# Sixty TensorE products into an unread PSUM bank behind the last product of a two-block transformer kernel

## What is computed

```python
def _sqrelu_mlp(h, w1, w2):
    return jnp.square(jax.nn.relu(h @ w1)) @ w2
...
        h = _rmsnorm_2(x, mlp_norm_g[layer])
        x = x + _sqrelu_mlp(h, mlp_w1[layer], mlp_w2[layer])
    return x
```

## Time and profile before

| | |
|---|---|
| median of 3 runs | 1064.75 us (1064.57 to 1065.28) |
| time of the profiled execution | 1063.91 us |
| its span, first to last instruction | 1062.1 us |
| granted TensorE clock, mean | 0.997 |
| TensorE busy with matmuls | 1044.7 us, 98% of the span |
| VectorE, ScalarE busy | 746.2 us, 548.7 us |

### The profile page before, as it was taken

How to read it: one execution, slowest core, us unless ns; L and a number is a source line. 1 busy time by engine, 2 the same in 40 slices (tenths; PEclk the granted TensorE clock), 3 DMA queues, 4 the chain that set the end, 5 groups by cost and what they waited for, 6 DMA issues and landing times.

```text
span 1062.1 us, 19331 instructions
## 1 busy us (share of the span) xinstructions
PE 1044.7 (98%) x7716; PEld 966.7 (91%) x7716; DVE 746.2 (70%) x810; ACT 548.7 (52%) x589; POOL 2.2 (0%) x5
## 2 busy tenths in 40 slices
PE   9999999999999999999999999999999999999998
PEld 7998897899999999989889999999898997888887
DVE  6855747768766666678767766666788987766673
ACT  6422536545644444465796444444576574454442
POOL 0000000000000000000000000000000000000000
PEclk8999999999999999999999999999999999999999
DMA  9794242345556666666416455456353444646531
GB/s 311 227 208 143 80 139 80 121 146 160 167 173 181 192 196 194 185 199 226 132 41 238 159 195 201 158 202 194 119 160 120 158 160 159 238 158 202 193 118 40
DMA packets 162589, 177.11 MB, mean 167 GB/s; under 512 B 4800, under 2 KB 148288, under 8 KB 162536
## 3 DMA queue, kind: packets, MB, share of 16 engines
q1 hardware_dynamic: 160704, 174.06, 51.3%
q10 hardware_dynamic: 1832, 2.30, 1.2%
HBM read 174.78 MB, written 1.57 MB: 166 GB/s over the span
## 4 chain that ended last, share of the span: by engine, by line
PE 82%; DVE 11%; ACT 4%; issue 1%; DMA 0%; SPq 0%; DVEq 0%; ACTq 0%
PE proj L466 38%; PE aux L910 13%; PE proj L476 10%; PE aux L932 8%; PE proj L475 5%; DVE wlo L1727 4%; DVE f L1727 2%; DVE f L1730 2%; ACT whi L1244 1%; DVE u L1730 1%; PE aux L663 1%; DVE x_all L1727 1%; PE aux L778 1%; PE aux L763 1%; PE aux L525 1%
## 5 line engine op out<-in xcount | busy, mean ns | idle before, releaser
L1727 DVE TENSOR_TENSOR wlo<-raw,whi 128x2048 fp32r<-128x2048 f32 (+2 forms) x179 | 374.7, 2093 | 99.8 <-ACT whi L1244 88.2
L466 PE MATMUL proj<-u,whi 128*128 128x256 f32 (+1 forms) x1888 | 346.9, 285 | 1.5 <-DVE u L1730 0.7
L1244 ACT ACTIVATE whi<-raw 128x2048 fp32r<-128x2048 f32 (+2 forms) x172 | 309.8, 1801 | 69.5 <-PE proj L466 43.2
L466 PEld LDWEIGHTS proj<-u,whi 128*128 128x128 f32 x1888 | 292.5, 189 | 8.3 <-issue 6.5
L466 PE MATMUL proj<-u,wlo 128*128 128x256 f32 (+1 forms) x944 | 266.8, 283 | 0.0
L476 PE MATMUL proj<-u,whi 128*128 128x512 f32 x512 | 179.9, 393 | 0.0
L466 PEld LDWEIGHTS proj<-u,wlo 128*128 128x128 f32 x944 | 179.1, 190 | 0.0
L910 PE MATMUL aux<-v,whi 128*128 128x256 f32 x864 | 155.2, 281 | 0.8 <-DVE v L1727 0.8
L475 PE MATMUL proj<-u,wlo 128*128 128x256 f32 x512 | 143.6, 281 | 0.9 <-DVE u L1730 0.9
L910 PEld LDWEIGHTS aux<-v,whi 128*128 128x128 f32 x864 | 133.3, 189 | 1.9 <-issue 1.2
L910 PE MATMUL aux<-v,wlo 128*128 128x256 f32 x432 | 121.1, 280 | 0.0
(11 more groups left out here) (307 smaller groups left out, 1065.4 us busy)
## 6 DMA issues: line engine op xcount, KB each, us to landing
raw<-in_mlp_w_dram SPq DMA_DIRECT2D x64, 1024.0 KB, 5.5
raw<-in_w_in_dram SPq DMA_DIRECT2D x21, 1024.0 KB, 7.0
raw<-in_od_w_in_dram SPq DMA_DIRECT2D x12, 1024.0 KB, 5.4
raw<-in_w_ffn_gate_dram SPq DMA_DIRECT2D x22, 512.0 KB, 3.9
raw<-in_w_ffn_up_dram SPq DMA_DIRECT2D x22, 512.0 KB, 5.2
raw<-in_w_ffn_down_dram SPq DMA_DIRECT2D x21, 512.0 KB, 5.4
raw<-in_ev_w_in_dram SPq DMA_DIRECT2D x10, 1024.0 KB, 5.2
raw<-in_w_ret_out_dram SPq DMA_DIRECT2D x4, 1024.0 KB, 5.1
```

The costliest lines, as they stand in the source:

```text
L466: ins = mm(o, w_of(a, k), x_of(b, k), start=first and k == 0 and j == 0, stop=last and k == kt - 1 and j == 2, skip_group_check=skip)
L1244: A.post(act(slot(whi, n, 0, wd), slot(raw, n, 0, wd), ACT.Copy), "hi_ready")
L1727: return ve.tensor_tensor(o, a, b, op)
```

## The change

Behind `hidden_layer(M1, 5)` TensorE's program calls a new function. It takes one block of 128 weights columns of the last chunk's `whi` as the stationary operand, and lets 256 columns of the high part of `u` stream past it, five times in each of twelve forms. All 60 products write the first 256 columns of bank 0 of `proj`. No semaphore is waited for or posted by them, and nobody reads the bank afterwards.

```diff
+            def orders_of_reading():
+
+                w = W(0, loop_last[2], 0, 2, D)[:, 0, 0:P]
+                flat = u[:, 0, :, :].rearrange("p k t -> p (k t)")
+                halves = lambda run: flat[:, 160:160 + S].rearrange("p (h a b) -> p a h b", h=2, b=run)
+                for moving in (flat[:, 16:16 + S], flat[:, 160:160 + S], flat[:, 160 + 128:160 + 128 + S], flat[:, 160 + 32:160 + 32 + S],
+                               flat[:, 160 + 8:160 + 8 + S], halves(2), halves(4), halves(16), halves(32),
+                               flat[:, 160:160 + 2 * S:2], flat[:, 160:160 + 2 * S].rearrange("p (a b) -> p a b", b=8)[:, :, 0:4],
+                               flat[:, 16:16 + S]):
+                    out = proj[:, 0, 0:S] if len(moving.shape) == 2 else (
+                        proj[:, 0, 0:S].rearrange("p (a b c) -> p a b c", a=moving.shape[1], b=moving.shape[2]) if len(moving.shape) == 4
+                        else proj[:, 0, 0:S].rearrange("p (a b) -> p a b", a=moving.shape[1]))
+                    for _ in range(5):
+                        mm(out, w, moving, start=True, stop=True, skip_group_check=True)
+
...
             hidden_layer(M1, 5)
+            orders_of_reading()
```

## The result

The changed kernel takes 1069.86 us (median of 3 runs, 1068.73 to 1070.42) against 1064.75: a ratio of 1.0046, 95% interval 1.0033 to 1.006, 5.1 us. The forecast was 1068.7 us, with a range of 1067.9 to 1071.9. The direction and the mechanism at the end of the program came out as forecast, and one term of the sum, what the forms add, was too small.

What follows compares the result with a forecast made beforehand. TensorE, busy 98%, bounds the kernel; behind its last product the copy and store hide 3.15 us. Sixty products at 0.118 us are 7.1 us, so 1064.75 + 3.9 = 1068.7 us, range 1067.9 to 1071.9.

Steps and rivals of the forecast that it cites:

- what the forms add: Scattered read orders in 30 of the 60 added products: taken as nothing, with ends of 0.7 us less and 3.2 us more.
- The place and the cover: Behind the last product, the copy and last store hide 3.15 us of TensorE work, some 27 of 60 products.
- The price of a plain product: Each added 256-column product behind the last one takes 0.118 us, the pace of the kernel's contiguous streams.
- The end: At the common end TensorE reports at 1065.82 us and the span ends at 1066.02 instead of 1062.1, +3.9 us.
- Case A: Every form of added product runs at the contiguous pace: 1068.7 us, own range 1067.9 to 1069.3; chance 0.58.
- Case B: Some added products' scattered reads waste part of each fetch: 1069.7 us, or 1071.9 with all halves too; chance 0.28.
- The Trainium skill on lines of 16 bytes: Moving operand reads: full rate when a line is hit twice in a row, so turns of two and step 2 cost nothing.
- C: The common end waits for TensorE's sequencer, not the array, so the 60 products vanish: 1064.75 us; chance 0.05 including cheap products.
- D: Behind the last product, instruction fetch or slow issue leaves the array dry; a 6 us stop gives 1070.7 us; chance 0.05.
- E: The changed length shifts something earlier in the program by a microsecond or two either way; chance 0.04.
- The second way of C: Added products cheap enough, under 0.088 us each, to stay within 0.2% of before; chance 0.05 together with an early-returning drain.

Runs made afterwards that it cites:

- the first sweep: Sixteen read orders of the moving operand, eight products each, added behind the kernel's last product; contiguous about 118 ns a product, scattered about 229.
- the sweeps: Five kernels, each run once, with 14 to 16 read or write orders, eight products each, behind the last product; only ns per product was read.
- the third sweep: Behind the last product, weights, output, 512-column and fp32 forms, eight products each; 512 columns at step 2 took 453 ns, weights at step 8 241 ns.

## Why the prediction was right, and where it was off

*The place and the cover.* Right. The end waits for TensorE's array: the drain ended within 0.1 us of the last product before, in the changed kernel and with 24 and 60 plain ones. Of 60 plain products (7.07 us) 3.2 us were hidden, of 24 (2.83 us) all, and of 60 ahead of the last call none.

*The price of a plain product.* Right: 7.07/60 = 0.118 us. No alignment of those in the changed kernel mattered. A start at an odd column, in the first sweep, costs 3 to 4 ns. The 109.2 ns that the prediction takes from the Trainium skill, "TensorE: Matmul & The Clock Gate", section "Back-to-back issue gap", did not hold for contiguous columns. The surplus of 9 ns goes with the order of reading: in turns of 1 the same product takes 111 ns, and one of 512 columns 216, which is what that formula for an isolated product gives.

*The end.* Right: 3.89 us measured for the plain 60 against 3.9.

*What the forms add.* This is the term that was mis-sized. The prediction took nothing for it; the 60 products last 7.97 us with the forms and 7.07 without, 0.90 us more, and the tails differ by 0.98. By the prices of the sweeps 5 x 52 ns are the turns of 2 (170 against 118), 5 x 10 the turns of 4 (128), and 5 x 111 every second column (229): 0.87 us. The reason given, that start and pace show only the number of columns, rested on rows that were all contiguous.

*Case A.* The forecast is this case, and its own range ended at 1069.3 us. The measured 1069.86 lies above it, inside the whole range only because that reaches up to case B.

*Case B.* In part it happened, near the price that B takes from the rows that are not fp32r for every second column (0.229 against 0.213 us), at half the surcharge for turns of 2, and not at all for four of eight columns. B's near end, 1069.7, is the closest of the cases to 1069.86, and partly by luck: it charges ten products for every second column and four of eight, and what happened was five of these, five turns of 2 and a little for turns of 4. The rows it took the price from count records and not products: a product that is not fp32r leaves two, as in the third sweep, so the eight of L611 are four products, and it is one record that costs twice the time of an fp32r product. Its surcharge of 0.107 us is also reckoned from 0.107 us for the columns alone, while the sum already had 0.118 for each product; from there it is 0.095, and the far end 1071.6. The mechanism given to B, fetches of which a part is wasted, is the family that the sweeps support, but the waste goes by side and by line.

*The Trainium skill on lines of 16 bytes.* The prediction's reading of "SBUF — State Buffer", section "Door 1: The DMA port swizzle", left 1068.7 with nothing for step 2, which touches each line twice in a row. The measured 229 ns speaks against two hits being enough for an fp32r stream, and two of four columns, also two hits a line, cost 229 as well. By the reading above each side takes only one column of the line.

*C, D, E.* Not seen: the drain did not return early, and the first added product starts 0.24 us behind the last down product, one pace of 512 columns. Nothing earlier moved: from the group of L604 to the end of the last down product it is 1024.5 us in both profiles. The second way of C, a product under 0.088 us, rested on 0.074 us for 128 columns. These eight records are four products (two loops of two in the kernel), so 0.148 us each, and the fp32r product of 128 columns takes about 107 ns in the third sweep: neither is under 0.088.

## What to carry to other kernels

In this kernel TensorE's work behind the last product was free up to the length of the last copy and store, and cost its full rest beyond it; the rows that say how much are the end of TensorE's drain and SP's arrival at the common end. A pace a few per cent above the columns' own time is a question worth asking even when TensorE is 98% busy: here it was the fetch of the moving operand, and an fp32r product of 256 columns read as two contiguous rows in turns ran 6% faster. Before such a gain is claimed, look in each layer for the engine that is second: in the feed-forward layer here the gain ended after 0.06 us of 8.5.

## What the runs showed of the hardware that was not expected

- An fp32r product of 256 columns takes 118 ns contiguous, 111 with two rows in turns of one column, 219 to 234 at steps 2 to 8; of 512 columns 229 to 231, 216 and 453; of 272 columns 126 contiguous and 116 in turns. Of 128 columns it takes about 107 contiguous, hardly less than 256 in turns.
- Four aligned columns of eight, twelve or sixteen take 115 to 121 ns, near the plain 118. Four of eight moved by one or two columns take 229 to 230 ns.
- Weights at step 2 cost 4 ns a product; their load lasts 196 ns instead of 188. At step 8 the load lasts 338 ns and a product takes 241.
- The output may go to two of four or four of eight columns of a bank, or in turns of 2, at no cost. The Trainium skill, "SBUF — State Buffer", section "Door 1: The DMA port swizzle", says that any non-contiguous access to PSUM slows matmuls; these three forms did not. All three write at least two neighbouring columns at a time; single ones were not tried.
- Open is why turns of 2, four in turns of 1 and fp32 in turns come out below the count of lines (170, 144 and 273 ns; by the fit a return costs 0.8 to 0.9 ns), and why turns of 4 take 128 ns where the count gives no more than contiguous columns.
